# Moving the compression work of a second transformer block in between its row-tile projections

## What is computed

```python
xn = _rms(x, norm1_g)
(gu, gv, q, kc, vc, ks_, vs_, kw, vw, ng, ca, cb, sB, sC, sh) = split(xn @ w_in)
# compression of keys and values, overlapping windows of 32 rows, stride 16 -> 31 windows
def compress(t, pe, w1, w2):
    blk = take(heads(t), cmp_idx) + pe           # 31 windows x 2 heads, 32 * 64 features
    hid = gelu(blk @ w1)                         # 2048 -> 128
    return hid @ w2                              # 128 -> 64
k_cmp = _rms(compress(kc, ...), k_g[0])
v_cmp = compress(vc, ...)
# then attention over compressed, selected and windowed keys, mixed by sigmoid(ng)
z = causal_depthwise_conv(ca * sigmoid(cb), 31 taps) ; y_c = silu(layernorm(z))
y_d = sB * causal_depthwise_conv(sC * sh, 3 taps)
```

## Time and profile before

| | us |
|---|---|
| median of 3 runs | 2322.45 (2320.39 to 2327.72) |
| the profiled execution | 2319.77 |
| its span, first to last instruction | 2317.9 |
| PE busy | 2056.6 (89%) |
| DVE busy | 1148.5 (50%) |
| ACT busy | 750.7 (32%) |
| mean granted clock of PE | 0.947 |

### The profile page before, as it was taken

One profiled execution on the slowest core, in us unless ns is written; L12 is line 12 of the kernel. 1 busy time (PEld: TensorE's weight loads), 2 busy tenths in 40 slices (PEclk: granted clock), 3 DMA queues, 4 the chain that ended last, 5 costly groups with the idle time before them and its releaser, 6 DMA issues.

```text
span 2317.9 us, 26283 instructions
## 1 busy us (share of the span) xinstructions
PE 2056.6 (89%) x9904; PEld 1387.7 (60%) x9904; DVE 1148.5 (50%) x2534; ACT 750.7 (32%) x1630; POOL 54.3 (2%) x96
## 2 busy tenths in 40 slices
PE   5888998999789697898998869878899996999999
PEld 2644655555444364565555427766578885887887
DVE  1285183645455638345656466874643444333333
ACT  2222223544431121233554213223533223222322
POOL 2000000000000100000000200000000000000000
PEclk9999999999899898999999888997999997999999
DMA  8011111010461211011010332222033331333231
GB/s 264 25 36 46 36 37 37 1 37 20 139 243 49 57 55 37 28 55 37 1 37 1 102 84 64 64 55 64 19 91 100 96 95 55 96 96 100 91 100 64
DMA packets 152685, 157.28 MB, mean 68 GB/s; under 512 B 5676, under 2 KB 114384, under 8 KB 152560
## 3 DMA queue, kind: packets, MB, share of 16 engines
q1 hardware_dynamic: 146672, 137.91, 19.5%
q0 software_dynamic: 5888, 17.68, 2.8%
HBM read 151.37 MB, written 4.19 MB: 67 GB/s over the span
## 4 chain that ended last, share of the span: by engine, by line
PE 70%; DVE 19%; ACT 5%; issue 3%; DMA 2%; POOL 1%; DVEq 0%; ACTq 0%; SPq 0%; POOLq 0%
PE psum L727 13%; PE psum L1164 9%; PE psum L1165 9%; PE psum L1166 9%; PE psum L739 5%; PE psum L902 5%; PE psum L754 5%; PE psum L935 3%; PE psum L916 3%; PE psum L690 2%; DVE stats L1922 2%; DVE arena L2179 2%; ACT arena L1428 1%; PE psum L772 1%; ACT arena L1261 1%
## 5 line engine op out<-in xcount | busy, mean ns | idle before, releaser
L727 PE MATMUL psum<-arena 128*128 128x512 f32 (+1 forms) x1280 | 473.5, 526 | 0.0
L1261 ACT ACTIVATE arena<-psum 128x384 f32<-128x384 f32 (+7 forms) x520 | 205.5, 423 | 751.2 <-PE psum L690 257.0
L1164 PE MATMUL psum<-part,part 128*128 128x512 f32 x992 | 389.8, 393 | 12.1 <-DVE part L2289 6.9
L1165 PE MATMUL psum<-part,part 128*128 128x512 f32 x992 | 389.1, 392 | 0.0
L1166 PE MATMUL psum<-part,part 128*128 128x512 f32 x992 | 388.8, 392 | 0.0
L727 PEld LDWEIGHTS psum<-arena 128*128 128x128 f32 x1280 | 246.4, 196 | 195.5 <-issue 177.7
L2285 DVE TENSOR_TENSOR part<-arena,part 128x1024 fp32r<-128x1024 f32 x112 | 137.2, 1226 | 251.7 <-ACT part L1261 251.7
L1261 ACT ACTIVATE part<-arena 128x1024 fp32r<-128x1024 f32 (+1 forms) x198 | 174.7, 914 | 212.6 <-PE psum L1166 149.2
L1164 PEld LDWEIGHTS psum<-part,part 128*128 128x128 f32 x992 | 187.9, 189 | 53.6 <-issue 13.8
L1922 DVE TENSOR_REDUCE stats<-psum 128x1 f32<-128x768 f32 (+6 forms) x208 | 138.8, 708 | 160.6 <-PE psum L902 159.3
L1166 PEld LDWEIGHTS psum<-part,part 128*128 128x128 f32 x992 | 187.9, 189 | 39.6
(11 more groups left out here) (266 smaller groups left out, 2038.2 us busy)
## 6 DMA issues: line engine op xcount, KB each, us to landing
arena<-in_w_in SPq DMA_DIRECT2D x75, 512.0 KB, 4.3
arena<-in_w_mlp SPq DMA_DIRECT2D x64, 512.0 KB, 3.9
arena<-in_w_ada SPq DMA_DIRECT2D x48, 512.0 KB, 6.1
arena<-in_w_gate SPq DMA_DIRECT2D x32, 512.0 KB, 4.0
arena<-in_w_out SPq DMA_DIRECT2D x24, 512.0 KB, 3.7
arena<-in_w_in SPq DMA_DIRECT2D x16, 256.0 KB, 3.2
arena<-in_w_branch SPq DMA_DIRECT2D x8, 512.0 KB, 4.0
arena<-in_x POOLq DMA_DIRECT2D x4, 512.0 KB, 9.0
```

What stands on the lines that cost most here:

```text
L727: mm = pe.matmul(bank(b)[:, c0:c1], lhs[:, k, m * P:(m + 1) * P], ring.view(tag, l, k // 2)[:, k % 2, c0:c1], start=k == 0, stop=k == kt - 1)
L1164: pe.matmul(dst, lo, x_hi_, start=first, stop=False)
L1165: pe.matmul(dst, hi, x_lo_, start=False, stop=False)
L1261: return act.activation(dst, src, ACT.Copy)
```

## The change

The two feature blocks of the compression are multiplied behind the four `gmlp` tiles (p = 3), in banks 6 and 7, and ACT and DVE make `blocks_c` there. The product with `w1` of the keys comes behind p = 8, with `w2` behind p = 9, DVE's norm behind p = 10, the turn behind p = 11; the values' products come behind p = 12 and 13. The tail is gone. The list of loads is put in the order of use. The splits of the four `gmlp` blocks come earlier within the features: two after features 6 and 7, one after feature 8, each ahead of that feature's taps; `q` and `kv` blocks are split at p = 3 to 7. No instruction is added or taken away.

```diff
@@ list_weights
     rows(("gmlp", 2), w, 0, 512)
+    for i, c in enumerate(FM2[:2]):
+        cols(("fm", i), w, c)
     rows(("q", 2), w, 512, 256, 4)
     rows(("kv", 2), w, 1024, 512)
-    rows(("ng", 2), w, 1536, P, 8)
-    ...
+    compression(0)
+    rows(("ng", 2), w, 1536, P, 8)
+    compression(1)
@@
-        SPLIT_2 = [("fm", i) for i in range(2, 12)] + [("gmlp", 2, i) for i in range(4)] + [("q", 2, i) for i in range(2)]
-        SPLIT_2 = SPLIT_2 + [("kv", 2, i) for i in range(4)] + [("fm", 0), ("fm", 1)]
+        SPLIT_2 = [("fm", i) for i in range(2, 12)] + [("gmlp", 2, i) for i in range(4)] + [("fm", 0), ("fm", 1)]
+        SPLIT_2 = SPLIT_2 + [("q", 2, i) for i in range(2)] + [("kv", 2, i) for i in range(4)]
-        SPLIT_AFTER = {0: (14,), 1: (15,), 4: (16,), 5: (17,), 6: (18,), 7: (19,), 9: (20,), 10: (21,)}
+        SPLIT_FEATURES = ((3,), (4,), (5,), (6,), (7,), (8,), (9, 10), (11, 12), (13,), ())
+        SPLIT_AFTER = {0: (14,), 1: (15,), 3: (16, 17), 4: (18,), 5: (19,), 6: (20,), 7: (21,)}
@@ PE
+            def compressed_2(p):
+                if p == 3:
+                    for i in range(2):
+                        feature_mm(i, 6 + i)
+                        bank_free(6 + i, [(fm_act, fm_dve)[i].at("read", i)])
+                if p in (8, 12):
+                    i = (p - 8) // 4
+                    b = 2 + i
+                    open_bank(b)
+                    pe.wait_ge(*fm_dve.at("blocks", i))
+                    ...   (16 matmuls with w1)
+                if p in (9, 13):
+                    ...   (w2, bank 2 + i, behind "hidden")
+                if p == 11:
+                    open_bank(2)
+                    pe.wait_ge(*cmp_dve.at("kc"))
+                    ...   (the turn of the compressed keys)
@@ PE rows_2
                     while due and due[0][0] <= p + 1:
                         later_2(due.pop(0)[1:])
+                    compressed_2(p)
                     yield True
@@ ACT, DVE features
-                    split_input_2(n + 3)
-                split_input_2(13)
+                    for j in SPLIT_FEATURES[n]:
+                        split_input_2(j)
@@ ACT compressed_2: p 3 the copies of fm 0, p 8 and 12 the Gelu, p 9 and 13 "compressed", p 11 the copy of kc
@@ DVE
+            def compressed_2(p):
+                if p == 3:
+                    for i in range(2):
+                        if i == 0:
+                            dve.wait_ge(*fm_act.at("read", 0))
+                        else:
+                            dve.wait_ge(*mm_done.at("weights", ring.number("fm", 1)))
+                            ...   (the copies of fm 1)
+                        dve.tensor_tensor(blocks_c[i], blocks_c[i], ..., ALU.add).then_inc(fm_dve(("blocks", i)), 1)
+                if p == 10:
+                    dve.wait_ge(*cmp_act.at("compressed", 0))
+                    head_rows_2(kc_rows[0:N_CMP, :], ...)
```

More of the change, by code:

```diff
@@ L204, in list_weights, with compression @@
     rows(("gmlp", 2), w, 0, 512)
+    for i, c in enumerate(FM2[:2]):
+        cols(("fm", i), w, c)
     rows(("q", 2), w, 512, 256, 4)
     rows(("kv", 2), w, 1024, 512)
-    rows(("ng", 2), w, 1536, P, 8)
-    for i, c in enumerate(FM2[:2]):
-        cols(("fm", i), w, c)
-    for i in range(2):
+    def compression(i):
         v = a["nsa_cmp_w1_2"][0, i].rearrange("(k p) e -> p k e", p=P)
@@ L1099, in later_2 @@
                     turn_rows(y_row, "row", m)
+            def compressed_2(p):
[8 more added lines that the diff above has]
+                    pe.wait_ge(*fm_dve.at("blocks", i))
+                    for k in range(16):
+                        if k % 8 == 0:
+                            pe.wait_ge(*ring.landed("w1", i, k // 8))
+                        mm = pe.matmul(bank(b)[:, 0:2 * N_CMP], ring.view("w1", i, k // 8)[:, k % 8, :], blocks_c[i][:, k, :], start=k == 0, stop=k == 15)
+                        if k % 8 == 7:
+                            mm.then_inc(mm_done(("weights", ring.number("w1", i, k // 8))), 1)
+                    bank_free(b, [cmp_act.at("hidden", i)])
+                if p in (9, 13):
+                    i = (p - 9) // 4
+                    b = 2 + i
+                    open_bank(b)
+                    for hh in range(2):
+                        mm = pe.matmul(bank(b)[0:N_CMP, hh * 64:(hh + 1) * 64], hid_c[:, i, hh * N_CMP:(hh + 1) * N_CMP], w2[i], start=True, stop=True)
+                    mm.then_inc(turn_done(("compressed", i)), 1)
+                    bank_free(b, [cmp_act.at("compressed", i)])
+                if p == 11:
+                    open_bank(2)
+                    pe.wait_ge(*cmp_dve.at("kc"))
+                    pe.transpose(bank(2)[:, 0:N_CMP], kc_rows[0:N_CMP, :], ident[0:N_CMP, 0:N_CMP]).then_inc(turn_done(("kc",)), 1)
+                    bank_free(2, [cmp_act.at("kc")])
             def rows_2():
@@ L1129, in block_2_inputs @@
                 run(rows_2())
[L1130 to L1155, removed]
             def attend_2():
@@ L1570, in later_2 @@
                     act.activation(y_row[:, m - 1:m + 1, :], y_row[:, m - 1:m + 1, :], ACT.Silu).then_inc(row2_act(("conformer silu", m - 1), ("conformer silu", m)), 1)
+            def compressed_2(p):
+                if p == 3:
+                    act.wait_ge(*mm_done.at("weights", ring.number("fm", 0)))
+                    for hh in range(2):
+                        src = bank(6)[64 * hh:64 * hh + 64, :].rearrange("p (n k s) -> p s k n", k=8, s=2)
+                        for s in range(2):
+                            for part_ in range(2):
+                                x = copy(blocks_c[0][64 * s:64 * s + 64, 8 * part_:8 * part_ + 8, hh * N_CMP:(hh + 1) * N_CMP], src[:, s, :, part_:part_ + N_CMP])
+                    x.then_inc(fm_act(("read", 0)), 1)
+                if p in (8, 12):
+                    i = (p - 8) // 4
+                    act.wait_ge(*mm_done.at("weights", ring.number("w1", i, 1)))
+                    act.activation(hid_c[:, i, 0:2 * N_CMP], bank(2 + i)[:, 0:2 * N_CMP], ACT.Gelu_apprx_tanh).then_inc(cmp_act(("hidden", i)), 1)
+                if p in (9, 13):
+                    i = (p - 9) // 4
+                    act.wait_ge(*turn_done.at("compressed", i))
+                    copy((kc_rows, v_cmp)[i][0:N_CMP, :], bank(2 + i)[0:N_CMP, 0:P]).then_inc(cmp_act(("compressed", i)), 1)
+                if p == 11:
+                    act.wait_ge(*turn_done.at("kc"))
+                    copy(kc_t, bank(2)[:, 0:N_CMP]).then_inc(cmp_act(("kc",)), 1)
             def rows_2():
@@ L1612, in block_2_inputs @@
                 run(rows_2())
[L1613 to L1627, removed]
             def attend_2():
@@ L2258, in block_2_inputs @@
                 alongside(rows_2(), 8, taps, 2 * (SCONV_K - 1) + 2 * (CONV_K - 1) - 48)
[L2259 to L2273, removed]
             def attend_2():
```

15 lines of the change are left out of this document (13 added, 2 removed).

## The result

The changed kernel took 2302.12 us (median of 4 runs, 2291.28 to 2302.79) beside 2322.41 us for the kernel before: a ratio over all runs of 0.9898, with a 95% interval of 0.9865 to 0.9932 (the two medians alone give 0.9913, because one of the four runs was 11 us faster than the rest). Two later sets of runs of the same kernel gave 0.9879 (0.9865 to 0.9894) and 0.9890 (0.9872 to 0.9908). The forecast was 2297, a ratio of 0.989; the first measurement lies where rival (a) put it, 2302.

The account below looks back on a forecast made before the run. PE was busy 89% of the span, but DVE's list of splits, taps and norms was taken to rule the rows. 20.0 us before attention plus 5 at its start gave 25.0, so 2297 us; range 2289 to 2308.

Parts of the forecast that it names:

- rival (a): Attention's first steps: the clock falls again or ACT sets their pace, leaving only the 20 us, 2302; chance 0.17.
- Part 1: First gmlp tile: early splits remove PE's waits of 4.08 and 2.81 us; the fourth tile ends about 10 us earlier.
- Part 2: Rows from p = 3: DVE's 8.0 us idle absorbs 2.3 and 5.3 us; last kv split at 1523.8, 0.4 us earlier.
- rival (b): DVE's list in the rows: idle times stay, the last kv split comes 7.6 us later, 2305; chance 0.12.
- Part 3: First kv tile to attention: 39.9 + 10.0 - 2.07 + 2.9 = 50.7 us; attention begins at 1577.7, 20.0 us earlier.
- Rival (c): Compression at p = 8 to 13 waits as it did in the tail, 5.9 us more, 2303; chance 0.07.
- Part 4: Attention's start: full-rate tiles in front give clock 1.00 in place of 0.50; 5 us gained, bounds 0 to 7.3.
- Rival (d): Mixing and hidden layer: PE spends a share at the 1.2 GHz level; slower, 2342 at 8%; chance 0.04.

Follow-up runs that it names:

- the one execution that kept 1.00: Profiled execution of the changed kernel plus nine extra 128x512 matmuls, results unread, in PE's three waits at attention's start; that kernel's median 2297.15 us.
- the two kernels whose waits were filled: Changed kernel plus nine matmuls at attention's start and thirty in the kv wait, 2297.17 us; changed kernel with q's norms late, kc's turn late and the nine, 2284.0 us.
- the nine extra matmuls: Nine 128x512 matmuls with unread results added in PE's three waits at attention's start; on the changed kernel alone 2297.15 us, beside 2297.47 unaltered.
- both moves: Changed kernel with q's two norms behind the last kv split and the compressed keys' turn behind p = 12; 2278.4 us without the nine matmuls, 2284.0 with.

## Why the prediction was right, and where it was not

- **Part 1, early splits.** Right. No wait in the first gmlp tile; moved back, both return with the very lengths, 4.08 and 2.81 us.
- **Part 2, DVE's list.** Right, and shown by undoing it: the last kv split was forecast to end at 1523.8 and ended at 1524.3, in a stage that began 0.9 us later. Fm 1 and ACT's copies came in time for DVE (its copies start at 1496.12 with no idle time ahead), so rival (b) is out.
- **Part 3, the way to attention.** Forecast 1577.7, measured 1576.56. Two small terms: a w1 product at full clock takes 3.68 us and not 4.58; the row that I took with "clock at 1.00 around it" (1579.52 to 1584.10) ran partly at 0.50, since the clock had fallen at 1582.2. And the wait for the compressed keys' norm is 2.66, not 2.9. The loads that I cost at nothing did cost nothing. Rival (c) is out: no w1 or w2 product waits for anything.
- **Part 4, attention's start: wrong.** The step that failed is "tiles at full rate stand in front", taken as reason enough for 1.00 behind it. PE did arrive at 1.00, and lost it at 1579.2, inside the third of three waits of 0.76, 0.32 and 1.32 us (the meeting of the engines, ACT's copy, ACT's table load and exponentials) with short products between them. It came back 27 us later, so the term was -3.7 in this profile and not +5; in the later one with 17 us at 0.50 (attention 70.4) it was -0.2. The kernel before had shown the same: behind two feature blocks at full rate and one wait of 1.33 us it fell 2.7 us into the first w1 product, long before attention:

```profile
1578.20:1582.20 4.00, 2.68 (x24) 2.71 (x25) 3.93 (x9) 0.00 (x0) 0.00 (x0) 1.00 0.47 135
1582.20:1598.95 16.75, 11.53 (x56) 10.29 (x55) 4.25 (x18) 1.62 (x7) 0.00 (x0) 0.50 0.40 112
```

The size of 5 was fair: the one execution that kept 1.00 had attention 4.3 us below before. The Trainium skill, TensorE: Matmul & The Clock Gate, Part 1, says that idle time brings the lower level back. The changed kernel's trace agrees so far, with the three waits just ahead of the fall; the two kernels whose waits were filled and whose clock fell all the same, behind 5.99 busy of 6.90 us and 6.19 of 7.10, show that the waits alone don't decide it. Nor did a busy PE get the higher level back soon: it was busy for nearly all of the 27 us at 0.50. Rival (a), to which I gave 0.17, is what happened.

- **The sum.** 20.0 + 5 = 25.0 was forecast; 21.4 - 3.7 - 0.9 is the 16.9 of the profiles, and the three sets of runs gave 20, 28 and 26 us. That the last two lie near 25 is luck as far as the 5 us go: no profile of the changed kernel shows attention gaining anything.
- **Rival (d), a lower clock in mixing,** is out: 200 us of mixing at 1.00 in the changed kernel as before.

What stays open: why the clock's stretch at 0.50 around the same wait is 7 us long in one execution and 20 in the next. The profiles show that it is, not what decides it. Also open is why the medians gained more than the profiles' stages do, and why the 5 us of the interleaved w1 products are in the profiles and not in the medians.

## What to carry to other kernels

Work can be put on an engine for nothing only as far as the list that bounds the stage has idle time, and here that list was DVE's, not PE's: find whose list the last wait ends on, add up its idle time, and compare it with what is put in. When the bound is such a list, look next for entries in it that nobody awaits yet: two norms that attention alone needed stood ahead of the splits that PE was waiting for, and moving them took 11 to 12 us off the stage with no other edit. And don't count on the clock of the stage behind: price its start both ways.

## What the runs showed of the hardware

The time at 0.50 in attention varied from none to 34 us between executions whose attention does the same work, but for the nine extra matmuls in three of the kernels. Without them attention takes 69.8 us with 14 us at 0.50, 70.2 to 70.4 with 17, 73.9 with 27 and 77.1 with 34; with them 65.9 us with none, 69.1 with 10 and 72.4 with 21. Over the whole range that is 0.3 to 0.4 us lost for each microsecond at 0.50, and not the half that a pure PE stretch would lose (the 128x512 matmuls of mixing's first rows step by 0.43 us at 0.50 and by 0.23 at 1.00); that ACT and DVE set part of the pace there would explain it, but was not tried by itself.

Low stretches lasted on while PE was busy: 26.85 of 27.10 us in the changed kernel, 20.50 of 20.50 with the nine matmuls on top of both moves. At the one kv wait of 7.5 us the stretch at 0.50 was 7 us long in most profiles, about 4 of it behind the wait, and 20 us in two, about 16 behind it, at a cost of 4.4 and some 6 us in the stage. Together with up to 8 us by which the stage's start differed, these can make up the spread of 5 to 13 us between the runs of one kernel; a gain of a few microseconds that a stage shows plainly can't be told from it.
